# Two transformer blocks on one core: running suffix sums in banks of their own, wide scores, rotary shuffles on DVE, and work moved to other places in the queues

## The reference

```python
# first block
h = rmsnorm(x); q, k, v = h @ w_qkv            # 4 differential heads, 8 stick-breaking heads
# differential: softmax(q1 k1 + bias) - lam * softmax(q2 k2 + bias), causal
# stick-breaking: per query, over keys from right to left
between = cumsum(log_1mb, reverse=True) - log_1mb     # log_1mb = log_sigmoid(-z), z = q k / 8
a = where(strict, exp(log_sigmoid(z) + between), 0); o = a @ v
x = x + rmsnorm(mix @ w_o)
x = x + rmsnorm((gelu(conv(h @ w_up)[gate]) * val) @ w_down)
# second block; six vectors sh, sc, gt = split(silu(c) @ w_mod + b_mod) shift, scale and gate it
h = modulate(rmsnorm(x)); q, k, v, f, g_a, g_f = h @ w_in
q, k = rope(q), rope(k)      # pairs of 16 channels are rotated
attn = softmax([q k_band, q k_ctx, sink]) @ [v, v_ctx]    # 3 key blocks of 128 and 256 context keys
x = x + gt1 * rmsnorm((sig(g_a) * attn @ w_pa + sig(g_f) * fft2(f) @ w_pf) @ w_out)
x = x + gt2 * rmsnorm((silu(conv(h2 @ w_up)) * gate) @ w_down)
```

## Time and profile before

| | |
|---|---|
| runs | 1392.53, 1394.49, 1396.64 us, median 1394.49 |
| profiled execution | 1394.65 us, span 1392.8 |
| PE busy | 1369.1 us, 98% |
| DVE, ACT busy | 839.2 (60%), 635.5 (46%) |
| chain that ended last | PE 89%, DVE 6%, ACT 3%, issue 1%, DMA 1% |

### The profile page before, as it was taken

One profiled execution on the slowest core, in us unless ns is written; L12 is line 12 of the kernel. 1 busy time (PEld: TensorE's weight loads), 2 busy tenths in 40 slices (PEclk: granted clock), 3 DMA queues, 4 the chain that ended last, 5 costly groups with the idle time before them and its releaser, 6 DMA issues.

```text
span 1392.8 us, 17279 instructions
## 1 busy us (share of the span) xinstructions
PE 1369.1 (98%) x6886; PEld 1113.9 (80%) x6886; DVE 839.2 (60%) x1272; ACT 635.5 (46%) x1032; POOL 26.9 (2%) x28
## 2 busy tenths in 40 slices
PE   9999999989999999999999999999999999999998
PEld 6777766788888888888987777887898888888887
DVE  6477897487766767665856444346566553444334
ACT  7435566654455434233635444444544333333234
POOL 3000000000003000000000000000000000000000
PEclk9999999999999999999999999999999999999999
DMA  6524220323223323664031111132213432323321
GB/s 236 202 92 136 76 71 26 132 107 121 91 91 100 98 92 126 208 224 152 31 131 61 47 60 61 61 121 91 92 59 124 150 106 91 105 92 94 103 91 61
DMA packets 46043, 146.71 MB, mean 105 GB/s; under 512 B 4971, under 2 KB 12139, under 8 KB 45580
## 3 DMA queue, kind: packets, MB, share of 16 engines
q1 hardware_dynamic: 45676, 145.08, 31.2%
q10 hardware_dynamic: 288, 0.52, 0.1%
HBM read 142.18 MB, written 3.41 MB: 105 GB/s over the span
## 4 chain that ended last, share of the span: by engine, by line
PE 89%; DVE 6%; ACT 3%; issue 1%; DMA 1%; SPq 0%; DVEq 0%; ACTq 0%
PE PS L353 26%; PE PS L355 25%; PE PS L354 25%; PE PS L1066 1%; PE PS L1057 1%; DVE mt L1723 1%; DVE wlo L319 1%; PE PS L568 1%; PE PS L1031 1%; DVE X L1729 1%; PE PS L1039 1%; PE PS L724 1%; PE PS L675 1%; PE PS L670 1%; PE PS L659 1%
## 5 line engine op out<-in xcount | busy, mean ns | idle before, releaser
L319 DVE TENSOR_TENSOR wlo<-raw,whi 128x1024 fp32r<-128x1024 f32 x205 | 252.3, 1236 | 341.7 <-ACT whi L303 341.2
L353 PE MATMUL PS<-Hhi,whi 128*128 128x512 f32 (+1 forms) x1136 | 434.8, 383 | 8.3 <-DVE Hlo L1729 6.4
L354 PE MATMUL PS<-Hlo,whi 128*128 128x512 f32 (+1 forms) x1136 | 423.9, 373 | 0.0
L355 PE MATMUL PS<-Hhi,wlo 128*128 128x512 f32 (+1 forms) x1136 | 423.9, 373 | 0.0
L303 ACT ACTIVATE whi<-raw 128x1024 fp32r<-128x1024 f32 x205 | 215.3, 1054 | 246.7 <-DMA raw<-in_w_down 119.5
L353 PEld LDWEIGHTS PS<-Hhi,whi 128*128 128x128 f32 x1136 | 215.4, 190 | 61.2 <-issue 15.4
L355 PEld LDWEIGHTS PS<-Hhi,wlo 128*128 128x128 f32 x1136 | 215.3, 190 | 38.1
L354 PEld LDWEIGHTS PS<-Hlo,whi 128*128 128x128 f32 x1136 | 215.5, 190 | 36.3 <-issue 1.4
L353 PE MATMUL PS<-Dhi,whi 128*128 128x512 f32 (+1 forms) x384 | 142.9, 372 | 0.0
L354 PE MATMUL PS<-Dlo,whi 128*128 128x512 f32 (+1 forms) x384 | 142.6, 371 | 0.0
L355 PE MATMUL PS<-Dhi,wlo 128*128 128x512 f32 (+1 forms) x384 | 142.6, 371 | 0.0
(11 more groups left out here) (410 smaller groups left out, 1832.9 us busy)
## 6 DMA issues: line engine op xcount, KB each, us to landing
raw<-in_w_up SPq DMA_DIRECT2D x88, 512.0 KB, 3.5
...
```

What stands on the lines that cost most here:

```text
L319: e.tensor_tensor(wlo[i % NS], raw[i % NS], whi[i % NS].bitcast(f32), ALU.subtract).then_inc(q["w_lo"], 1)
L353: e.matmul(o, lhs[0], rhs[0], start=first, stop=False, skip_group_check=own)
L354: e.matmul(o, lhs[0], rhs[1], start=False, stop=False, skip_group_check=own)
L355: return e.matmul(o, lhs[1], rhs[0], start=False, stop=last, skip_group_check=own)
```

## The change

- Start: the first halves of the first four weight chunks are loaded, copied and subtracted first, the second halves later; five warm-up matmuls; the small matmuls for the norm and lambda go together before the last bank.
- `sb_sums` keeps the sums of a head pair in banks 2 and 3 over its four key blocks: the block that was the triangle's a step ago gets the rest (`restr` = ones − triangle, so both make ones), the new one the triangle. All logits go to banks 0 and 1.
- Columns of group 3 leave tick 14 for the place before the first up projection; groups 10 and 11 leave block 2's up projection for the place before it, and their loads and DVE parts move into the out projection.
- Rope turns its operand with a DVE shuffle; no permutation matmul and no `permc`.
- Scores of block 2: one matmul per head for 256 own and 256 context keys, and one of 128 for a third block.
- Output: 8 stores of 256 KB.

```diff
     trir = at("trir", "G", 11264, [128, 128], f32r)
-    onesr = at("onesr", "G", 11776, [128, 128], f32r)
+    restr = at("restr", "G", 11776, [128, 128], f32r)
...
+    KK = at("KK", "A", 8192, [128, 2048])
+    K2 = KK[:, 0:T]
...
-            if i == 0:
-                e.dma_start(raw[0][:, 0:512], source(0)[:, 0:512]).then_inc(q["raw_first"], 16)
-                e.dma_start(raw[0][:, 512:1024], source(0)[:, 512:1024]).then_inc(q["raw0"], 16)
+            if i < 4:
+                e.dma_start(raw[i][:, 512:1024], source(i)[:, 512:1024]).then_inc(q[f"raw{i}"], 16)
...
-    PAIR, _uses = {}, []
+    PAIR_FREE, _last = {}, ("qk_ev", 2)
     for t in range(16 + LAG):
-        for name, s, sem in (("z", t, "sb_z"), ("a", t - 1, "sb_a"), ("d", t - LAG, "d_l")):
+        for name, s, sem in (("z", t, "sb_z"), ("d", t - LAG, "d_l")):
             if 0 <= s < 16:
-                PAIR[name, s] = (2 * (len(_uses) % 2), _uses[-2] if len(_uses) > 1 else ("qk_ev", 2 + 2 * len(_uses)))
-                _uses.append((sem, s + 1))
+                PAIR_FREE[name, s] = _last
+                _last = (sem, s + 1)
...
-    T_COLUMNS = {9: 2, 14: 3}
+    T_COLUMNS = {9: 2}
...
-        load_to(e, ld, 1)
-        e.dma_start(vec[:, ng:NV], a["vec"][:, ng:NV]).then_inc(q["l_vec"], 16)
-        load_to(e, ld, 2)
-        const("ones", ones, *CCOL["ones"])
-        load_to(e, ld, 4)
+        for i in range(4):
+            e.dma_start(raw[i][:, 0:512], source(i)[:, 0:512]).then_inc(q[f"raw_o{i}"], 16)
         for i in range(1, 4):
             e.dma_start(X[:, 2 * i:2 * i + 2, :], a["x"][:, 2 * i:2 * i + 2, :]).then_inc(q[f"l_x{i}"], 16)
+            load_to(e, ld, i)
+        load_to(e, ld, 4)
+        e.dma_start(vec[:, ng:NV], a["vec"][:, ng:NV]).then_inc(q["l_vec"], 16)
+        const("ones", ones, *CCOL["ones"])
...
-        load_to(e, ld, CH["w_f2"])
+        load_to(e, ld, CH["w_q3"])
         e.wait_ge(q["kvc_mm"], 2)
-        e.dma_start(permc, a["consts"][:, CCOL["perm"][0]:CCOL["perm"][1]]).then_inc(q["l_c2"], 16)
...
-        load_to(e, ld, CH["w_up2"] + 6 + NS)
-        for n in range(42, 48):
-            load_to(e, ld, CH["w_up2"] + 6 + 2 * (n - 41) + NS)
-            mod_load(e, n)
+        for o, ns in enumerate(((42, 43), (44,), (45, 46), (47,))):
+            load_to(e, ld, CH["w_out2"] + o + NS)
+            for n in ns:
+                mod_load(e, n)
         load_to(e, ld, NCHUNK)
-        for c in range(8):
-            e.wait_ge(q["x_new"], XN[3] + c + 1)
-            e.dma_start(out[:, c, HALF["a"]], X[:, c, HALF["a"]]).then_inc(q["l_out"], 16)
-        for c in (0, 1, 2, 3, 4, 6, 5, 7):
+        for c in range(0, 8, 2):
+            e.wait_ge(q["x_new"], XN[3] + c + 2)
+            e.dma_start(out[:, c:c + 2, HALF["a"]], X[:, c:c + 2, HALF["a"]]).then_inc(q["l_out"], 16)
+        for c in (0, 2, 6, 4):
             if c < N_PE:
-                e.wait_ge(q["x_out"], c + 1)
+                e.wait_ge(q["x_out"], c + 2)
             else:
-                e.wait_ge(q["x_new"], XN[3] + 8 + c - N_PE + 1)
...
-        for _ in range(3):
+        for _ in range(5):
             e.matmul(PS[:, 7, 0:384], G_r[:, 0:128], G_r[:, 0:384], start=True, stop=True)
 
         for k in range(0, 4, 2):
             for j in range(4):
-                if k == 0 and j == 0:
-                    e.wait_ge(q["w_lo_first"], 1)
-                elif k == 0:
-                    e.wait_ge(q["w_lo"], j + 1)
+                if k == 0:
+                    e.wait_ge(q["w_lo_first"], j + 1)
                 for i in range(k, k + 2):
                     if j == 0:
                         e.wait_ge(q["h_lo"], i + 1)
                     products(e, PS[:, j, :], wtile(j, i), hx(i), i == 0, False)
 
         for j in range(4):
-            if j == 1:
+            if j == 3:
                 e.wait_ge(q["l_ones"], 16)
+                e.wait_ge(q["x_acc"], 7)
+                e.matmul(PS[:, 7, :], ones, G_s, start=True, stop=True).then_inc(q["stat"], 1)
                 e.wait_ge(q["setup"], 4)
                 e.matmul(PS[:, 6, 0:2], ones, lprod, start=True, stop=True).then_inc(q["lam_mm"], 1)
-            if j == 3:
-                e.wait_ge(q["x_acc"], 7)
-                e.matmul(PS[:, 7, :], ones, G_s, start=True, stop=True).then_inc(q["stat"], 1)
+            e.wait_ge(q["w_lo"], j + 1)
...
         def sb_sums(s):
             j, kb, w = sb_geom(s)
-            b, free = PAIR["a", s]
             e.wait_ge(q["sb_lo"], s + 1)
-            e.wait_ge(q[free[0]], free[1])
+            e.wait_ge(q["sb_a" if s else "qk_ev"], s or 4)
             for h in range(2):
+                if kb < 3:
+                    for i in range(2):
+                        e.matmul(PS[:, 2 + h, 128 * kb + 128:T], restr, lparts(j, kb + 1)[i][:, h, :], start=False,
+                                 stop=False, skip_group_check=True)
                 for i in range(2):
-                    last = e.matmul(PS[:, b + h, 0:w], trir, lparts(j, kb)[i][:, h, :], start=i == 0,
-                                    stop=kb == 3 and i == 1)
-                for jb in range(kb + 1, 4):
-                    o = 128 * (jb - kb)
-                    for i in range(2):
-                        last = e.matmul(PS[:, b + h, o:w], onesr, lparts(j, jb)[i][:, h, :], start=False,
-                                        stop=jb == 3 and i == 1)
+                    last = e.matmul(PS[:, 2 + h, 128 * kb:T], trir, lparts(j, kb)[i][:, h, :], start=kb == 3 and i == 0,
+                                    stop=i == 1, skip_group_check=True)
             last.then_inc(q["sb_tri"], 1)
...
+        acc_columns(3, 5, 0)
         e.wait_ge(q["p_y"], 10)
...
-        def rope(i, x):
-            e.wait_ge(q["qk2_ev"], i + 1)
-            if i:
-                e.wait_ge(q["rp"], 3 * (i - 1) + 1)
-            else:
-                e.wait_ge(q["l_c2"], 48)
-                e.wait_ge(q["kvc_ev"], 2)
-            e.matmul(PS[:, 5, :], permc, x, start=True, stop=True).then_inc(q["rp_mm"], 1)
...
-            masks = [(0, mlowb)] * (qb > 0) + [(128 * (nl - 1), mhighb)] * (qb < 3)
+            masks = [(0, mlowb)] * (qb > 0) + [(128 if nl == 2 else 512, mhighb)] * (qb < 3)
+            seg = 1024 - 128 * k0
+            own_and_context = KK[:, 128 * k0:128 * k0 + 2 * seg].rearrange("p (a b) -> p a b", a=2)[:, :, 0:256]
             if p == 0:
                 e.wait_ge(q["bm_cc"], 3)
                 e.wait_ge(q["qk2_ev"], 4)
@@ -1028,18 +1017,16 @@
             e.wait_ge(q["rp"], 3 * j + 6)
             qq = [Q2[64 * h:64 * h + 64, j, 128 * qb:128 * qb + 128] for h in range(2)]
             for h in range(2):
-                e.matmul(flat[h][:, 0:128 * nl], qq[h], K2[64 * h:64 * h + 64, 128 * k0:128 * (k0 + nl)],
+                e.matmul(flat[h][:, 0:512].rearrange("p (a b) -> p a b", a=2), qq[h], own_and_context[64 * h:64 * h + 64],
                          start=True, stop=False)
+            if nl == 3:
+                for h in range(2):
+                    e.matmul(flat[h][:, 512:640], qq[h], K2[64 * h:64 * h + 64, 128 * (k0 + 2):128 * (k0 + 3)],
+                             start=True, stop=False)
             for h in range(2):
-                for i, (o, m) in enumerate(masks):
-                    e.matmul(flat[h][:, o:o + 128], identb, m, start=False,
-                             stop=i == len(masks) - 1)
-            for c0, c1 in [(0, 256)] if nl == 2 else [(0, 128), (128, 256)]:
-                for h in range(2):
-                    last = e.matmul(flat[h][:, 128 * nl + c0:128 * nl + c1], qq[h], KC[64 * h:64 * h + 64, c0:c1],
-                                    start=True, stop=True)
-                    if c1 == 256:
-                        last.then_inc(q["a_qk"], 1)
+                for o, m in masks:
+                    last = e.matmul(flat[h][:, o:o + 128], identb, m, start=False, stop=True)
+                last.then_inc(q["a_qk"], 1)
...
+        acc_columns(10, 5, 0)
+        acc_columns(11, 5, 8)
         e.wait_ge(q["p_y"], PY[3])
...
+        def first_lo(i):
+            e.wait_ge(q["w_hi_first"], i + 1)
+            tt(wlo[i][:, 0:512], raw[i][:, 0:512], whi[i][:, 0:512].bitcast(f32), ALU.subtract, "w_lo_first")
+
         for c in range(8):
             if c == 0:
-                e.wait_ge(q["w_hi_first"], 1)
-                tt(wlo[0][:, 0:512], raw[0][:, 0:512], whi[0][:, 0:512].bitcast(f32), ALU.subtract, "w_lo_first")
+                first_lo(0)
                 e.wait_ge(q["l_gain"], 16)
             e.wait_ge(q["h_hi"], c + 1)
             stt(Hlo[:, c, :], X[:, c, :], vc("g_pre1", c), Hhi[:, c, :].bitcast(f32), ALU.mult, ALU.subtract, "h_lo")
             if c == 1:
-                split_to(4)
+                for i in range(1, 4):
+                    first_lo(i)
+            elif c in (3, 5, 7):
+                split_to(c // 2)
+        split_to(4)
...
+        tt(restr, ones, tri, ALU.subtract, "rest")
...
```

(48 more changed lines are left out.)

78 lines of the change are left out of this document (33 added, 45 removed).

## The result

The changed kernel took 1379.67 us (median of 4 runs, 1377.33 to 1380.05) against 1394.36 of the kernel before (median of 4 runs, 1392.53 to 1396.64): 0.9894 of it, 95% interval 0.9882 to 0.9906, so 14.7 us or 1.06% faster. The forecast was 1377.1 in a range from 1370.5 to 1387.

What follows compares the result with a forecast made beforehand. The prediction took TensorE, busy for 98% of the span, to bound the kernel. Its eight terms summed to 17.5 us, taken from 1394.65 to give 1377.1, in a range from 1370.5 to 1387.

Steps and rivals of the forecast that it cites:

- R1: Tick loop: ACT and DVE hold the ticks, what the sums free is waited back, their gain falls to 1: 1381; chance 0.12.
- R2: Rope: the shuffles or their place cost more than the matmuls, the rope gain goes to 0: 1380.5; chance 0.12.
- R3: Start held by DVE and loads, gaining 0.5, and low clock stays behind block 2's gap: 1381; chance 0.15.
- Term 1: Start: first halves first and two more warm-up matmuls bring full clock sooner, 2.5 us won (0.5 to 3.2).
- Term 2: Tick loop: running suffix sums save matmuls, partly waited back in j=3; net 4.6 us won (2.5 to 5.4).
- Term 8: Output: 4 fewer store issues on SP, less than half of 1.9 taken; 0.8 us won (0.5 to 1.1).
- Term 5: Block 2's scores: wider matmuls save 0.22 on eight two-key-block and 0.11 on eight three-key-block steps; 2.6 us (1.8 to 3.4).
- term 3: Tick 14: moving its columns out wins only 0.2 us, as PE falls back on the wait for ACT's Z.
- R5: Ticks: one pair of banks for all logits makes PE stand for DVE in every tick: 1400, slower; chance 0.04.
- Term 4: Rope: five permutation matmuls saved, 4.3, less 1.0 of wait at the second scores; net 3.3 us (1.5 to 4.3).
- Terms 6 and 7: Block 2's up projection: columns moved into the wait before it, 1.8 us; full clock behind that gap, 1.7, 7 in 10.

Runs made afterwards that it cites:

- full_sums: Changed kernel, with the sums of every step made from all blocks again in banks 2 and 3, logits still in banks 0 and 1: 1382.89 us.
- tick14: Changed kernel, with the columns of group 3 back in tick 14: 1378.79 us in one run.
- warm3: Changed kernel, with three warm-up matmuls in place of five: 1383.38 us in one run.
- adds_late: Changed kernel, with POOL's seven adds of squares held until the start's last Hlo, and ACT's last scaled x ahead of its waits for POOL: 1380.67 us in one run.
- stats_first: Changed kernel, with the maximum of block 2's first scores taken on DVE ahead of two weight subtractions: 1376.09 us once, then 1375.94.
- columns_back: Changed kernel, with the column matmuls of groups 10 and 11 and their bias back in the second up projection: 1384.42 us in one run.
- last_store: Changed kernel, with the last store of 256 KB made as two of 128 KB: 1381.97 us in one run.

## Why the prediction was right, and where it was off

The direction, the total and the kind of each gain were right: 15.2 of 17.5 in the profile. Five terms were mis-sized, and R1, R2 and R3 were there in part. That the total is off by 2.3 only is in part luck: terms 1, 2 and 8 came out 3.1 too large together and term 5 1.4 too small; the misses of all terms, without their signs, are 5.1.

**Term 2 was too large (4.6, measured 3.1 with term 3).** The step that failed is "Net 4.6": only j=3 was to wait its saving back. The count of matmuls and their price held nearly: full_sums gives 5.0 for the matmuls saved, where 5.4 was forecast. But in j=0 0.48, the saving of kb=1, went into the wait for VD, in j=2 0.87 into dq, and in j=3 0.38 into dnv (0.54 was forecast there, for DT). I had read the spare time of scores alone, not that of the products whose bank an eviction has to clear. That is R1 at under half its price of 3.6. R5, the shared pair, is refuted by full_sums, which has the pair and is as far ahead of the kernel before at the end of the ticks as at their start. Term 3 had the right size for a wrong reason: the wait was for dnr and not for Z (tick14).

**Term 1 (2.5, measured 1.7).** The clock part was right (warm3: 2.74 at 18.57), though not by its own steps: the five warm-up matmuls ended at 6.60 and not at 8.0, since they stood 0.64 apart until 4.67 and 0.33 from 5.14 on, and TensorE then waited 0.98 for Hlo. In adds_late they stood 0.64 apart up to 7.23, and the products began at 7.66 with the same spacing. The term's lower bound named what took the rest: Hlo at 1.40 to 1.78 beside POOL, and a wait of 0.62 at 21.39. adds_late shows that POOL's adds are the cause; holding them cost more than it won. "SBUF — State Buffer" ("Who interferes with whom") in the Trainium skill says that the two engines lock each other out there; the durations, 0.75 for DVE and 1.29 for POOL apart and 1.78 and 1.55 together, agree in kind, though neither grew by the other's whole length.

**Term 4 (3.3, measured 3.0).** The five matmuls gave what was forecast, 4.4. A shuffle took 0.73 to 0.75, up to 0.07 over the value taken; the estimate of 0.6, scaled by elements from the Trainium skill's figure ("VectorE: DVE Perf Modes", "Rules for kernel authors"), was lower than measured. The constants came early (699.08) and w_q3's wlo ended at 705.97, before its product. The wait at the second scores was 1.4 and not 1.0. stats_first shows its place: three subtractions ahead of the maximum. It is not the ropes, which were done at 716.8, after which DVE was idle for 2.36 until Ft came from ACT.

**Term 5 (2.6, measured 4.0)** lay outside its own bounds (1.8 to 3.4), and it failed on the steps with three key blocks. The forecast had 1.71 for one; the rows give 754.19 − 752.70 = 1.49, and four of the eight took 1.61, so they gained 0.33 or 0.21 each and not 0.11. The set of 512 took 0.96 to its successor (753.66 − 752.70) and not 1.06, the set of 128 with all masks 0.53 and not 0.65. The eight steps with two key blocks gave 1.7 together, as forecast. Terms 4 and 5 have no run of their own: their sizes are read from the rows alone.

**Terms 6 and 7** held: 1.7 and 1.5. columns_back brought the half clock back.

**Term 8 (0.8, measured 0.2).** The four issues took 2.32 in place of 3.77, so 1.45 less (the forecast had 1.9). The first of them stood 0.44 later behind the last product, since a store now waits for two chunks of X, and the span ended 2.55 behind the last issue in place of 1.7: a store of 256 KB took 2.2 to land (median) where one of 128 KB had taken 1.7. last_store tells that smaller stores at the end give nothing more: the two of 128 KB landed in 2.3 there.
